# Turning five of six convolution pieces to token form: TensorE and ScalarE, or VectorE's 32x32 blocks and SyncE's transfers

## What is computed

```
p = h @ w_in                       # columns q_g, k_g, v_g: 1024 each
qkv = silu(causal_conv(qkv, w))    # width 4, each channel by itself, along the tokens
q = l2norm(q) * 128 ** -0.5        # for each token and head of 128 channels
k = l2norm(k)
o = gated_delta_chunked(q, k, v, beta, g)
```

## Time and profile before

| | us |
|---|---|
| median of 3 executions | 2191.46 |
| lowest, highest | 2191.05, 2192.14 |
| the profiled execution, its time | 2190.68 |
| its span, first to last instruction | 2189.4 |
| TensorE busy | 2154.0 |
| VectorE busy | 1516.8 |
| ScalarE busy | 1007.7 |

### The profile page before, as it was taken

One profiled execution on the slowest core, in us unless ns is written; L12 is line 12 of the kernel. 1 busy time (PEld: TensorE's weight loads), 2 busy tenths in 40 slices (PEclk: granted clock), 3 DMA queues, 4 the chain that ended last, 5 costly groups with the idle time before them and its releaser, 6 DMA issues.

```text
span 2189.4 us, 27127 instructions
## 1 busy us (share of the span) xinstructions
PE 2154.0 (98%) x10352; PEld 1809.5 (83%) x10352; DVE 1516.8 (69%) x1901; ACT 1007.7 (46%) x1268; POOL 25.5 (1%) x26
## 2 busy tenths in 40 slices
PE   6899999999999999999999999999999999999998
PEld 5799998888888888888888888888888888888887
DVE  8988798999887677755555555576546665655656
ACT  5357355443444644443444434464444444444444
POOL 0001000000000000000000000000000000000000
PEclk9999999999999999999999999999999999999999
DMA  9975568898898589976667666666666766667663
GB/s 404 420 286 162 191 211 282 301 316 270 276 348 294 205 280 321 309 232 192 203 203 207 199 195 205 193 203 191 189 196 188 211 202 205 200 194 205 220 193 125
DMA packets 315537, 515.93 MB, mean 236 GB/s; under 512 B 93288, under 2 KB 108944, under 8 KB 309904
## 3 DMA queue, kind: packets, MB, share of 16 engines
q1 hardware_dynamic: 315408, 514.21, 71.9%
HBM read 503.10 MB, written 2.12 MB: 231 GB/s over the span
## 4 chain that ended last, share of the span: by engine, by line
PE 86%; DVE 7%; DMA 3%; ACT 2%; issue 1%; POOL 0%; DVEq 0%; ACTq 0%; POOLq 0%
PE bank L1295 26%; PE bank L1297 26%; PE bank L1296 26%; DVE WL L2113 3%; PE bank L1479 1%; PE bank L1302 1%; PE bank L1303 1%; PE bank L1304 1%; DVE RAW L2100 1%; PE bank L1227 1%; DVE A L2290 1%; ACT WH L1556 1%; DMA RAW<-in_w_ada_dram 1%; DMA RAW<-in_w_cd_dram 1%; DMA A<-in_w_cq_dram 1%
## 5 line engine op out<-in xcount | busy, mean ns | idle before, releaser
L2113 DVE TENSOR_TENSOR WL<-RAW,WH 128x1024 fp32r<-128x1024 f32 x706 | 859.9, 1223 | 556.6 <-ACT WH L1556 547.7
L1556 ACT CAST WH<-RAW 128x1024 fp32r<-128x1024 f32 x706 | 738.4, 1049 | 880.6 <-PE bank L1297 718.1
L1295 PE MATMUL bank<-WH,HTh 128*128 128x512 f32 x1922 | 754.3, 392 | 0.8 <-DVE WL L2113 0.8
L1297 PE MATMUL bank<-WH,HTl 128*128 128x512 f32 x1922 | 748.4, 389 | 0.0
L1296 PE MATMUL bank<-WL,HTh 128*128 128x512 f32 x1922 | 747.9, 389 | 0.0
L1295 PEld LDWEIGHTS bank<-WH,HTh 128*128 128x128 f32 x1922 | 360.9, 188 | 75.9 <-DVE WL L2113 1.7
L1297 PEld LDWEIGHTS bank<-WH,HTl 128*128 128x128 f32 x1922 | 360.8, 188 | 75.8
L1296 PEld LDWEIGHTS bank<-WL,HTh 128*128 128x128 f32 x1922 | 361.1, 188 | 73.2
L1295 PE MATMUL bank<-WH,R2h 128*128 128x512 f32 x408 | 160.2, 393 | 0.3 <-DVE WL L2113 0.3
L1297 PE MATMUL bank<-WH,R2l 128*128 128x512 f32 x408 | 158.9, 390 | 0.0
L1296 PE MATMUL bank<-WL,R2h 128*128 128x512 f32 x408 | 158.9, 389 | 0.0
(11 more groups left out here) (305 smaller groups left out, 1793.6 us busy)
## 6 DMA issues: line engine op xcount, KB each, us to landing
RAW<-in_a_w_in_dram SPq DMA_DIRECT2D x192, 512.0 KB, 4.2
RAW<-in_w_gate_up_dram SPq DMA_DIRECT2D x176, 512.0 KB, 4.6
RAW<-in_w_ada_dram SPq DMA_DIRECT2D x128, 512.0 KB, 5.5
RAW<-in_w_in_dram SPq DMA_DIRECT2D x112, 512.0 KB, 5.1
RAW<-in_w_down_dram SPq DMA_DIRECT2D x88, 512.0 KB, 4.4
RAW<-in_a_w_out_dram SPq DMA_DIRECT2D x64, 512.0 KB, 4.3
A<-in_w_ada_dram SPq DMA_DIRECT2D x17, 1024.0 KB, 14.0
RAW<-in_w_o_dram SPq DMA_DIRECT2D x32, 512.0 KB, 6.5
```

The costliest lines, as they stand in the source:

```text
L1295: e.matmul(o, ah[:, s], hi[:, k, :], start=first, stop=False)
L1297: i = e.matmul(o, al[:, s], hi[:, k, :], start=False, stop=last)
L1556: e.copy(hi, rv).then_inc(S["hi"], 1)
L2113: e.tensor_tensor(lo, rv, hi.bitcast(F32), ALU.subtract).then_inc(S["lo"], 1)
```

## The change

Pieces 0 to 4 are no longer turned by `nat` but by a generator `nat_turn`; piece 5 stays. `nx_t` turns CV in 32x32 blocks on VectorE into a new tile NQ. `nx_s` issues four transfers of 32 KB in each of four slots, which put the blocks straight into NAT, with no copy behind. NAT's axes are in another order, so that a destination is eight runs of 32 elements for each partition. A piece is begun when the one before it is done, and `cells` waits as before. The first piece's turn gates the convolution of piece 2, as `nat` did. The result of the inversion, XO, lies in two tiles now and is written by two additions. The diff, cut:

```diff
-        self.NAT = {k: ar(8 * i, 2048).rearrange("p (b h d) -> p b h d", b=2, h=8) for i, k in enumerate("qkv")}
+        self.NAT = {k: ar(8 * i, 2048).rearrange("p (h b d) -> p b h d", b=2, h=8) for i, k in enumerate("qkv")}
+        self.NQ = ar(96, 1024)
-        self.XO = ar(12, 512).rearrange("p (n i) -> p n i", i=32)
+        self.XO = [x.rearrange("p (n i) -> p n i", i=32) for x in (self.ROPE[:, 128:384], self.place("XO1", 256))]
-FF_TURNED, Y_TURNED = range(10), range(6)
+FF_TURNED, Y_TURNED, NAT_TURNED = range(10), range(6), 5
# opening(), slot 10 and from slot 14 on
             if c == 3:
-                self.put_nat(0)
+                self.bg.append(self.nat_turn(0))
...
-        self.put("nat_sq", 0, self.ms(), self.ms())
-        m = self.ms_n
         yield
         yield
-        self.put_nat(1)
-        self.put("nat_n", 0, m)
-        self.have.add(("nat", 0))
-        yield
-        yield
-        self.put("nat_sq", 1, self.ms(), self.ms())
...
+        while ("nat", 0) not in self.have:
+            yield
+        self.bg.append(self.nat_turn(1))
+
+    def nat_turn(self, n):
+        self.sx_of["nat", n] = len(self.sx_of) + 1
+        self.put("nx_t", n)
+        self.have.add(("nat_t", n))
+        yield
+        for tq in range(4):
+            self.put("nx_s", n, tq)
+            yield
+        for _ in range(2):
+            yield
+        if n < 4:
+            self.put("nat_sq", n, self.ms(), self.ms())
+            m = self.ms_n
+            yield
+            yield
+            self.put("nat_n", n, m)
+        self.have.add(("nat", n))
# conv_rest(n), n = 2 to 5
+        if n < NAT_TURNED:
+            while ("nat", n - 1) not in self.have:
+                yield
+            self.bg.append(self.nat_turn(n))
+            return
# VectorE
+        elif kind == "nx_t":
+            n, = args
+            W.wait_ge(*(("cv_th", n + 1) if n in SILU else ("cv_s", cv_scaled(n) + 1)))
+            if n:
+                W.wait_ge("sx_in", 256 * n)
+            else:
+                W.wait_ge("cs", NG)
+            e.transpose(L.NQ, L.CV[n % 2]).then_inc(S["sx_t"], 1)
...
-            e.tensor_tensor(L.XO.rearrange("p n i -> p i n"), L.XF[:, :, 0, :], L.XF[:, :, 1, :], ALU.add).then_inc(S["inv"], 1)
+            for g in range(2):
+                ns = slice(8 * g, 8 * g + 8)
+                e.tensor_tensor(L.XO[g].rearrange("p n i -> p i n"), L.XF[:, :, 0, ns], L.XF[:, :, 1, ns], ALU.add
+                                ).then_inc(S["inv"], 1)
# SP
+        elif kind == "nx_s":
+            n, tq = args
+            W.wait_ge("sx_t", n + 1)
+            W.wait_ge("ht_lo", NG)
+            for dq in range(4):
+                d = slice(32 * dq, 32 * dq + 32)
+                src = L.NQ[d, :].rearrange("p (n q d) -> p n q d", q=4, d=32)[:, :, tq, :]
+                dst = L.ar(8 * (n // 2), 2048)
+                dst = dst[32 * tq:32 * tq + 32, :].rearrange("p (n d) -> p n d", d=P)[:, 8 * (n % 2):8 * (n % 2) + 8, d]
+                e.dma_start(dst, src).then_inc(S["sx_in"], 16)
# ScalarE: nat_sq waits for the transfers
-                W.wait_ge("nat_c", 2 * n + bb + 1)
+                W.wait_ge("sx_in", 256 * (n + 1))
```

More of the change, by code:

```diff
@@ L792, in opening @@
         self.have.add("kpt")
-        self.put("nat_sq", 0, self.ms(), self.ms())
-        m = self.ms_n
         yield
         yield
-        self.put_nat(1)
-        self.put("nat_n", 0, m)
-        self.have.add(("nat", 0))
-        yield
-        yield
-        self.put("nat_sq", 1, self.ms(), self.ms())
-        m = self.ms_n
-        yield
[L805 to L812, removed]
+        while ("nat", 0) not in self.have:
[3 more added lines that the diff above has]
+        self.sx_of["nat", n] = len(self.sx_of) + 1
+        assert len(self.sx_of) == n + 1
+        self.put("nx_t", n)
+        self.have.add(("nat_t", n))
+        yield
+        for tq in range(4):
[10 more added lines that the diff above has]
+        self.have.add(("nat", n))
     def q_rest(self):
@@ L835, in conv_rest @@
         self.have.add(("nat_t", n))
[L836 to L842, removed]
         self.have.add(("nat", n))
@@ L1392, in pe_program @@
             four(bank[b], [cv[:, i * T + bb * P:i * T + bb * P + P] for i in range(4)]).then_inc(S["nat_t"], 1)
-            held[b] = [("nat_c", 2 * n + bb + 1)]
+            held[b] = [("nat_c", bb + 1)]
         elif kind == "cell":
@@ L1486, in pe_cell @@
         W.wait_ge("nat", 8)
-        W.wait_ge("nat_c", 12)
+        W.wait_ge("nat_c", 2)
+        W.wait_ge("sx_in", 256 * NAT_TURNED)
         turned(b, k).then_inc(mine, 1)
@@ L1698, in act_program @@
             W.wait_ge("half", job_end(sch, "conv", n))
-            W.wait_ge("nat_t", 2 * n - 2)
+            if n > 1:
+                W.wait_ge("sx_t", n - 1)
             for q in range(2):
@@ L1719, in act_program @@
             W.wait_ge("ht_lo", NG)
-            W.wait_ge("nat_t", 2 * n + bb + 1)
+            W.wait_ge("nat_t", bb + 1)
             e.copy(L.NAT["qqkkvv"[n]][:, bb, 4 * (n % 2):4 * (n % 2) + 4, :],
@@ L2631, in spread_blocks @@
     def spread_blocks(dst, rows):
-        n = 8 * g + 4 * tt
+        n = 4 * tt
         e.tensor_tensor(dst.rearrange("p h (q c) -> p h q c", c=32),
@@ L2661, in dve_cell @@
     elif name == "X":
-        W.wait_ge("inv", 67)
+        W.wait_ge("inv", 68)
         W.wait_ge(own, CELL["dve", 1, "atm"] if tt == 0 else CELL["dve", 0, "n2"])
-        spread_blocks(XT, L.XO)
+        spread_blocks(XT, L.XO[g])
         if tt == 0:
@@ L2838, in sp_program @@
             W.wait_ge("sx_t", m)
-            if m > 1:
+            if m - 1 in sch.sx_free:
                 W.wait_ge(*sch.sx_free[m - 1])
```

## The result

The changed kernel takes **2212.2 us** (median of five, 2208.55 to 2212.76) against 2191.46: ratio 1.0091, 95% interval 1.0076 to 1.0105. It is slower by 20 us where 2.6 were forecast, and above the range's 2200.5. The profiled execution took 2208.55 us, 17.9 more than that of before; the traces account for this one.

What follows compares the result with a forecast made beforehand. TensorE was taken to set the time, with VectorE just in time. -3.3 (pieces 0 to 2) + 3.2 (pieces 3 and 4) + 2.7 (b jobs' end) = +2.6 us, giving a median of 2194.1 us; range 2187.5 to 2200.5.

Steps and rivals of the forecast that it cites:

- signs set beforehand: Expected: TensorE waits 3 to 5 us for VectorE at 290 to 330 us, 2.7 at 608; no VectorE gaps at 290 to 320.
- the b jobs' end: Slots 145 to 147, left without matmuls by cells four slots later: TensorE waits for a ScalarE and VectorE chain, +2.7 us.
- slower rival: At piece 4, transfers delay weight loads by SP's whole 4.6 us: 2197.7 us, 2200 with landing times stretched; chance 0.30.
- Pieces 0 to 2: Slots 10 to 18, up to 205 us: six transpose groups (2.64 us) and a 0.63 us wait go, -3.3 us.
- Piece 2's convolution moves from slots 10 and 11 to 12 and 13, because it waits for piece 0: Step in the first stretch's new order; no cost was booked for it.
- The list of leads: How long weight halves are ready before TensorE needs them: mostly 2 us and more, 0.06 at half 79, 2.2 at 83.
- The lead grows by more than TensorE gains, so I book the whole: Up to slot 21 VectorE loses more work than it gets, so the full -3.3 us was booked.
- Pieces 3 and 4: Slots 40 to 60, 278 to 340 us: VectorE's order makes TensorE 2.2 us later, plus 1.0 for loads: +3.2 us.
- SP and the DMA engines: Transfers delaying weight loads at pieces 3 and 4: bounds nothing and 4.6 us (all of SP's lateness), 1.0 taken.
- The loads in question are used ...: Ground for the lower bound on load delay: loads are used three to four slots later, after cells' VectorE work left.
- The 4 to 5 us of the DMA engines: Full bandwidth a piece's transfers would take: some 0.3 of the engines for 13 us, from two measured windows.
- The inversion: VectorE's inversion is moved four slots, not lengthened: booked 0, bounds -0.3 and +1.2 us.

Runs made afterwards that it cites:

- e1: Changed kernel with piece 0's turn started one slot earlier, so piece 2's convolution keeps its former slots: 2209.3 us, ratio 1.0074.
- e11: Kernel before, nothing added, with squares and norms of pieces 1 and 2 moved to slots 29, 31, 40 and 42: 2193.44 us, ratio 1.0011.
- e7: Kernel before with inversion and cells four slots later, plus 80 dummy transfers issued by SP in the change's slots: 2200.7 us, ratio 1.0044.
- e6: Changed kernel with every DMA of the turn cut to 2 of its 32 partitions, a sixteenth of the bytes: 2211.1 us, ratio 1.0085.
- e3: Kernel before with only the inversion, the cells and what hangs on them four slots later: 2197.03 us, ratio 1.0024.
- e5_tight_conv2: Changed kernel, piece 2's convolution in its former slots, each piece's turn allowed once the previous piece's transfers are issued: 2203.01 us, ratio 1.0050.
- e15: Kernel before with late cells and the extra transfers on SP as 8 DMAs of 64 KB a piece, not 16 of 32 KB: 2201.0 us, ratio 1.0043.

## Why the prediction was wrong

Three of the signs set beforehand came. TensorE waited 4.5 us for VectorE between 290 and 330 us (3 to 5 forecast), VectorE showed no gap at 290 to 320 us, and the wait at the b jobs' end was 2.54 us (2.7 forecast). The sign of the slower rival came too: ScalarE waited 12.4 us for weights between 330 and 350 us, 2.0 before. Most of the miss lies where no sign was set, ahead of 290 us and behind 350 us. Two steps failed above all: what the moved convolution and piece 0's transposition do before half 45 (+2.8 and not -3.3), and what the transfers do to the loads behind half 87 (+4.7 and not +1.0).

**Pieces 0 to 2, booked at -3.3.** What was to be saved was: -1.6 us at half 37 (piece 0's two groups and the stall of 0.63, which stands ahead of both: the four matmuls at 168.97 are another step's and are still there) and another -2.0 between halves 42 and 45. The failed step is the sentence "Piece 2's convolution moves from slots 10 and 11 to 12 and 13, because it waits for piece 0", from which nothing was drawn. The move is right; what it does to the banks' next user, 4.14 us and the clock behind it, was not looked up. Shown by the trace, and by e1, where it goes. The stretch is +2.8 and not -3.3: 6.1 us of the miss. Undoing the move (e1) gives back 2.2 of them. The other 3.9 fail a second step, the one next quoted: e1 still stands at +0.5 because VectorE's transposition comes ahead of splits without lead. The list of leads named halves 79 and 83 and left out half 44, which has 0.0 us in the kernel before.

**"The lead grows by more than TensorE gains, so I book the whole".** False at halves 37 to 39, where the lead fell by 1.6 us, and in e1 up to half 44. True in the changed kernel from half 40 up to attention, mostly because TensorE had been made to wait (5 us and more at halves 45 to 51), and of no use: TensorE passes attention without reference to splits, since it waits there for copies of L2265 that stand in VectorE's program behind the moved norms.

**Pieces 3 and 4, +3.2.** The mechanism, VectorE's order, was right and put at half 79 and 83. Its size was counted from slot 40 on; it began at half 65, in slot 38 (+1.0, behind piece 2's transposition, which e11 doesn't have), and went on at half 71 (+1.9, which e11 has too). Measured from half 45 to 86: +4.0 in place of 2.2. Of that, 2.5 to 2.8 was shown by e11 to need only the moved norms.

**SP and the DMA engines, 1.0 (0 to 4.6).** Measured by e7 alone: 4.7 us by half 129, just past the upper bound that I left aside (3.4 at the end, 3.7 by the medians). "The loads in question are used ... from half 87 on, where the cells' VectorE work has left" is the failed step: in e7 nothing waits at half 87, but the lead is spent, and is missed later, 1.2 us by half 100 and 3.5 us from half 103 to 129. The 4 to 5 us of the DMA engines that the prediction worked out for a piece from two windows are not what was paid: e6, with a sixteenth of the bytes, is as slow.

**The inversion, booked at 0 (-0.3 to +1.2).** The +1.2 was booked "if the lead were full before it": it was not. Late cells alone cost nothing there (e3), with the transfers 3.0 (from half 103 to 127 in e7's and the changed kernel's traces, 3.1 and 3.0).

**The b jobs' end, +2.7.** Right in place, chain and size (2.54 of waiting). With the halves at 154 to 170 and, in e3, the clock, late cells are worth 4.9 us by the medians, not 2.7.

The terms now, by traces: first stretch +2.8; attention and pieces 3, 4 to half 86 +3.9; from there, beyond what late cells do, +6.3, less 1.2 behind half 129, mostly for a clock that did not fall at the end; late cells +6.0: 17.8. Of the +6.3, 4.7 is e7's. The rest, 1.6, may come from the changed kernel entering this stretch with less lead (half 89 at 0.0 for 3.8), which no run took apart. Open too: the medians' difference is 20.7 us, 3 above that of the traces. The changed kernel's five times spread over 4.2 us, before's five over 1.1, but its 14 beside e1 over 3.0; the profiled execution was the changed kernel's fastest. A clock that falls longer in one execution than in the next could do that, but e1, whose clock stays at 1.00 in that stretch, spreads as widely, and no run took it apart.

The slower rival was the right one in sign and in place, but its ground is not shown: bytes don't decide it (e6), landing times no run changed by themselves, and most of the loss lies outside it.

## What to carry to other kernels

When a step moves in a hand-made order, list for each resource it holds (a bank, a buffer, a place in an engine's program) who takes it next and when, before any saving is booked; here the one line not followed up cost 6.3 us where it fell, more than all transposes were worth. Removing a wait is no gain by itself either: with the stall at the b jobs' end closed, two halves further on waited for their weights. An in-order engine's spare time is not where its busy share is low but where nothing waits behind it; and a lead used up unseen is paid where the next stretch needs it. A transfer's cost to its issuing queue counts apart from its bytes, and its latency must fit between the steps on both sides of it: a chain made longer by 15 us pushes everything behind it.

## What was not expected of the hardware

TensorE's clock: after a wait of 4.14 us it was granted at 0.50 for the next 4.6 us of matmuls; after a wait of 2.54 us it fell in one kernel (e3_before_late, 0.50 at 613.5 to 615 us) and not in another (the changed one), and after one of 1.90 us it fell in e5_tight_conv2 (0.50 at 273 to 275 us). A stall on TensorE can thus be dearer than its length, by 2.2 us in the first case.

SyncE's time for a DMA of 128-byte rows: 0.65 us for 2 KB as for 32 KB, and 0.64 for 64 KB as long as the DMA engines kept up, 1.1 to 1.6 when they were full. Here it bought nothing to make such a transfer smaller (e6), and next to nothing to make it larger (e15).
